# Delta-net heads: tiles in the order q, k, v, z, convolution taps read from PSUM, two value heads solved in turn, x normalised before its split

## The reference, cut to what matters

```
h      = rms_norm(x, norm_g)                      # x * rsqrt(mean x^2 + eps) * gain, per token
proj   = h @ dn_w_in                              # q, k (12 heads), v, z (24 heads), a, b, xq
qkv    = silu(causal_depthwise_conv(proj[q,k,v])) # 4 taps along the tokens, per channel
q, k   = l2_norm(q) / sqrt(128), l2_norm(k)       # each q/k head serves two value heads
g,beta = -exp(a_log)*softplus(a+dt), sigmoid(b)
o      = gated_delta_rule(q, k, v, g, beta)       # per value head: a unit lower triangular
                                                  # system per chunk, then a scan over chunks
mix    = rms_norm(o, out_g)
xa     = memory_cross_attention(xq, rms_norm(mem) @ w_kv)      # 4 heads
x      = x + (concat[mix, xa] * silu(z)) @ w_out
second layer: rms_norm, an mLSTM (4 heads), an HGRN (8 heads), out, a gated embedding, rms_norm
```

## Time and profile before

| what | us |
|---|---|
| median of 3 runs (range) | 3907.66 (3907.61 to 3908.97) |
| the profiled execution's own time | 3906.5 |
| its span, first to last instruction | 3904.6 |
| PE busy | 3431.5 (88%) |
| DVE, ACT, POOL busy | 1650.8, 782.0, 1839.2 |
| mean granted clock of PE | 0.949 |
| memory tiles (PE) | 36.1 to 140.1 |
| tile W_AB (PE) | 182.6 to 194.1 |
| cross-attention tiles | 210.4 to about 434 |
| first six delta tiles end | 500.3 |
| `natural` of head 0, head 1, head 11 starts | 506.4, 647.8, 1979.1 |
| end of `head_out` of head 11 (PE) | 2117.6 |
| tile W_GATE ends, first mLSTM tile starts | 2449.0, 2468.6 |

### The profile page before, as it was taken

One profiled execution on the slowest core, in us unless ns is written; L12 is line 12 of the kernel. 1 busy time (PEld: TensorE's weight loads), 2 busy tenths in 40 slices (PEclk: granted clock), 3 DMA queues, 4 the chain that ended last, 5 costly groups with the idle time before them and its releaser, 6 DMA issues.

```text
span 3904.6 us, 46749 instructions
## 1 busy us (share of the span) xinstructions
PE 3431.5 (88%) x17262; PEld 2836.3 (73%) x17262; DVE 1650.8 (42%) x2050; ACT 782.0 (20%) x1129; POOL 1839.2 (47%) x1828
## 2 busy tenths in 40 slices
PE   7789988898898889888969999799998888869897
PEld 6567777787777778777848777677776666648685
DVE  2422245544544553555352122334446565541433
ACT  3321122212211221222130001111122222220111
POOL 5444633433433433343324666466664444427574
PEclk9999999999999999999989999899999999989998
DMA  4312211111111111111122323122221111132222
GB/s 159 135 71 86 81 60 65 54 46 60 61 48 52 64 54 48 59 54 64 48 98 92 134 87 139 62 90 91 97 103 62 62 64 62 56 127 94 78 86 86
DMA packets 53362, 306.67 MB, mean 79 GB/s; under 512 B 5012, under 2 KB 7188, under 8 KB 21812
## 3 DMA queue, kind: packets, MB, share of 16 engines
q1 hardware_dynamic: 33984, 247.48, 18.0%
q10 hardware_dynamic: 19316, 58.32, 4.0%
HBM read 284.74 MB, written 21.04 MB: 78 GB/s over the span
## 4 chain that ended last, share of the span: by engine, by line
PE 72%; DVE 19%; issue 3%; ACT 3%; POOL 1%; DMA 1%; ACTq 0%; DVEq 0%; SPq 0%; POOLq 0%
PE gemm_ps L382 18%; PE gemm_ps L384 17%; PE gemm_ps L383 17%; DVE arena L761 14%; DVE arena L767 4%; PE bankA L494 4%; PE bankC L506 3%; PE bankB L504 2%; PE bankA L667 2%; ACT arena L1384 1%; POOL w_lo L340 1%; DVE a_lo L761 1%; PE bankA L529 1%; PE bankB L518 1%; PE bankA L513 1%
## 5 line engine op out<-in xcount | busy, mean ns | idle before, releaser
L382 PE MATMUL gemm_ps<-a_hi,w_hi 128*128 128x512 f32 (+1 forms) x3744 | 1512.6, 404 | 90.5 <-DVE a_lo L761 72.9
L355 POOL CAST w_hi<-w_raw 128x512 fp32r<-128x512 f32 x880 | 565.6, 684 | 1969.5 <-issue 1950.6
L383 PE MATMUL gemm_ps<-a_lo,w_hi 128*128 128x512 f32 (+1 forms) x3744 | 1452.0, 388 | 0.0
L384 PE MATMUL gemm_ps<-a_hi,w_lo 128*128 128x512 f32 (+1 forms) x3744 | 1451.3, 388 | 0.0
L340 POOL TENSOR_TENSOR w_lo<-w_raw,w_hi 128x512 fp32r<-128x512 f32 x944 | 1281.5, 1388 | 53.3 <-ACT w_hi L1384 53.3
L382 PEld LDWEIGHTS gemm_ps<-a_hi,w_hi 128*128 128x128 f32 x3744 | 719.5, 192 | 254.3 <-DVE a_lo L761 67.4
L384 PEld LDWEIGHTS gemm_ps<-a_hi,w_lo 128*128 128x128 f32 x3744 | 716.1, 191 | 145.3
L383 PEld LDWEIGHTS gemm_ps<-a_lo,w_hi 128*128 128x128 f32 x3744 | 718.8, 192 | 133.5 <-issue 9.9
L761 DVE TENSOR_TENSOR arena<-gemm_ps,arena 128x512 f32<-128x512 f32 (+3 forms) x234 | 157.5, 673 | 1043.5 <-PE gemm_ps L384 1018.7
L1384 ACT ACTIVATE arena<-arena 128x512 f32<-128x512 f32 (+5 forms) x418 | 252.3, 604 | 915.7 <-DVE arena L761 888.1
L761 DVE TENSOR_TENSOR arena<-arena 128x256 f32<-128x256 f32 (+3 forms) x444 | 331.8, 747 | 80.0 <-ACT arena L1618 43.6
(11 more groups left out here) (136 smaller groups left out, 2021.9 us busy)
## 6 DMA issues: line engine op xcount, KB each, us to landing
w_raw<-w_stream SPq DMA_DIRECT2D x236, 1024.0 KB, 4.8
y_scratch<-arena ACTq DMA_DIRECT2D x20, 512.0 KB, 3.2
arena<-y_scratch ACTq DMA_DIRECT2D x15, 512.0 KB, 3.6
arena<-gc_scratch ACTq DMA_DIRECT2D x12, 512.0 KB, 3.6
arena<-x_t ACTq DMA_DIRECT2D x1, 4096.0 KB, 15.3
arena<-y_scratch ACTq DMA_DIRECT2D x1, 4096.0 KB, 24.3
x_scratch<-arena ACTq DMA_DIRECT2D x1, 4096.0 KB, 12.1
y_out<-arena ACTq DMA_DIRECT2D x4, 1024.0 KB, 3.9
```

The costliest lines, as they stand in the source:

```text
L355: pool.tensor_copy(part(w_hi, w, q), part(w_raw, w, q)).then_inc(pool_step, 1)
L382: pe.matmul(o, hi, a_hi[:, k, 0:width], start=(k == 0), stop=False)
L383: pe.matmul(o, hi, a_lo[:, k, 0:width], start=False, stop=False)
L384: last = pe.matmul(o, lo, a_hi[:, k, 0:width], start=False, stop=(k == KT - 1))
```

## The change

1. **Loop order and weights of the steps.** The tiles of a head come as q, k, v, v, z, z (`stream`). `DN_STEPS` has new weights, `natural` is split (the transposes of v are a step `values` of their own, behind `gate` and all four `silu`; `natural` itself waits only for q and k and for `o_root` of the head before), and each level is four steps of weight 0.75: `half` and `whole` of value head 0 and of value head 1 in turn, with ACT copies of 128x512 and COPY_PREDICATED of 128x512. `head_out` starts at part 68 in place of 79. `qd` is made at the end of DVE's `natural`.
2. **Read-out.** For q, k, v ACT reads the PSUM tile and writes it times the last tap into `cv`; DVE adds three taps with SCALAR_TENSOR_TENSOR that read PSUM directly (`raw`, its copy and the TENSOR_SCALAR are gone); only then is the bank `evicted`; ACT's `Silu` follows. Tile q's first ACT copy waits for `pm_ready` of the solve beside it. z (here and in cross attention) is read by ACT's `Silu` straight from PSUM. `z_g` is a copy of `z_in` at the trip's end. The Sqrt table is asked for early in two places.
3. **x.** It is loaded after the memory's squares; its 16 squares (ACT) and their running sum `root` (DVE) go among memory tiles 7 to 14; one matmul with ones into bankC, root and reciprocal follow after the last memory tile; `fill(1)` multiplies gain and reciprocal root in one operation, so tiles of this layer need no `rstd` (`copied` in place of `scaled`). `square_sums(1)` is gone.
4. **Row transposes.** L421 and its copy move from behind W_AB to `q_norm` of the first cross-attention head; L597 and its copy from behind W_GATE to behind the first eight mLSTM tiles, and there PE waits for the copy.

```diff
-DN_STEPS = ([("natural", 14), ("transposed", 6)]
-            + [(s, l, g) for l in range(1, LEVELS) for s, g in (("half", 2.5), ("whole", 4))]
-            + [("solved", 4)]
-            + [(s, n, g) for n in range(NB) for s, g in (("rest", 2), ("output", 2))]
-            + [("head_out", 17)])
+X_FROM = 7
+DN_STEPS = ([("natural", 10), ("values", 8), ("transposed", 6)]
+            + [(s, l, a, 0.75) for l in range(1, LEVELS) for s in ("half", "whole") for a in range(2)]
+            + [("solved", 6)]
+            + [(s, n, g) for n in range(NB) for s, g in (("rest", 2), ("output", 3))]
+            + [("head_out", 28)])
...
-        ort, yo = halves(o_ + 5 * 1024), halves(o_ + 6 * 1024)
+        ort, yo = halves(o_ + 3 * 1024), halves(o_ + 5 * 1024)
...
+        def level_count(j, l, a):
+            return 2 * ((LEVELS - 1) * j + l - 1) + a + 1
...
+            pe.wait_ge(s["x_acc"], KT)
+            pe.matmul(bankC[:, 1, :], ones, root, start=True, stop=True).then_inc(s["sq_summed"], 1)
...
-            pe.wait_ge(s["kv_root"], XH)
-            square_sums(1)
             for k in range(KT):
                 gemm(W_AB, 0, k, 1)
-            pe.wait_ge(s["rows_ready"], 1)
...
                 if step[0] == "natural":
-                    pe.wait_ge(s["silu"], 4 * j + 4)
+                    pe.wait_ge(s["o_root"], 2 * j + 2)
+                    pe.wait_ge(s["silu"], 4 * j + 2)
...
+                elif step[0] == "values":
+                    pe.wait_ge(s["gate"], j + 1)
+                    pe.wait_ge(s["silu"], 4 * j + 4)
...
                 elif step[0] == "half":
+                    l, a = step[1:3]
+                    if l > 1:
+                        pe.wait_ge(s["lvl"], level_count(j, l - 1, a))
...
                 elif step[0] == "whole":
+                    pe.wait_ge(s["t1_sbuf"], level_count(j, l, a))
...
             ml_trip(0, None, mix=False)
+            pe.wait_ge(s["g_x"], 4)
...
+            last.then_inc(s["g_rowsT"], 1)
+            pe.wait_ge(s["mcols_ready"], 1)
             with pe.Fori(0, MLH - 1) as j:
...
                 scaled(kv[:, c, :], W_MEM, c, width=M)
+                if X_FROM <= c < X_FROM + KT // 2:
+                    for k in range(2 * (c - X_FROM), 2 * (c - X_FROM) + 2):
+                        v.wait_ge(s["squared"], KT + k + 1)
+                        if k == 0:
+                            op(v.tensor_copy, root, sqr[:, 0, :], sem=s["x_acc"], value=1)
+                        else:
+                            op(v.tensor_tensor, root, root, sqr[:, k % 2, :], ALU.add, sem=s["x_acc"], value=k + 1)
+            v.wait_ge(s["root_ready"], 2)
+            op(v.reciprocal, root, root, sem=s["rstd_ready"], value=2)
...
+            fill(1, src0, C_NORM, scale=root)
...
             def dn_evict(c, g):
-                scaled(raw[:, 3:T + 3], W_DN, c, g, 6)
-                o = cv[:, c - 2, :]
-                tap = 4 * (c - 2)
-                op(v.tensor_scalar, o, raw[:, 0:T], cw[:, tap:tap + 1], None, ALU.mult)
+                v.wait_ge(s["tapped"], 4 * g + c + 1)
+                tap = 4 * c + 3
                 for t in range(1, 4):
-                    op(v.scalar_tensor_tensor, o, raw[:, t:t + T], cw[:, tap + t:tap + t + 1], o, ALU.mult, ALU.add,
-                       sem=s["conv"] if t == 3 else None, value=4 * g + c - 1)
+                    o = cv[:, c, t:T]
+                    op(v.scalar_tensor_tensor, o, gemm_ps[slot][:, 0:T - t], cw[:, tap - t:tap - t + 1], o,
+                       ALU.mult, ALU.add, sem=evicted[slot] if t == 3 else None, value=n + 1)
...
                 elif step[0] == "whole":
+                    if l < LEVELS - 1:
+                        copy_after(v.copy_predicated, X[:, a, :, :], low[:, l:l + 1, :].to_broadcast([P, NB, P]),
+                                   quad(bankB)[:, a, :, :])
+                    copy_after(v.copy_predicated, XT[:, a, :, :], lowT[:, l:l + 1, :].to_broadcast([P, NB, P]),
+                               quad(bankC)[:, a, :, :], sem=s["lvl"], value=level_count(j, l, a))
...
+            act.dma_start(src0, xT).then_inc(s["src_loaded"], 16)
+            act.wait_ge(s["sq_summed"], KT)
+            for t in range(2, W_AB):
+                high_tile(t)
+                if X_FROM <= t < X_FROM + KT // 2:
+                    act.wait_ge(s["src_loaded"], 32)
+                    for k in range(2 * (t - X_FROM), 2 * (t - X_FROM) + 2):
+                        if k >= 2:
+                            act.wait_ge(s["x_acc"], k - 1)
+                        op(sqr[:, k % 2, :], src0[:, k, :], ACT.Square, s["squared"], KT + k + 1)
+            act.wait_ge(s["x_acc"], KT)
+            act.wait_ge(s["sq_summed"], KT + 1)
+            op(root, bankC[:, 1, :], ACT.Sqrt, s["root_ready"], 2, bias=eps[:, :], scale=1.0 / D)
...
             def gates(g):
+                op(z_g[:, :, :], z_in[:, :, :], ACT.Copy, s["gate"], g + 1)
+                act.preload_act_table(ACT.Sqrt)
...
                 elif step[0] == "half":
+                    act.wait_ge(s["t1"], level_count(j, l, a))
+                    if (l, a) == (1, 0):
+                        act.wait_ge(s["dy_stored"], 16 * j + 16)
+                    op(T1[:, a, :, :], quad(bankA)[:, a, :, :], ACT.Copy, s["t1_sbuf"], level_count(j, l, a))
                 elif step[0] == "head_out":
+                    act.preload_act_table(ACT.Sqrt)
                     act.wait_ge(s["o"], j + 1)
...
             def dn_trip(g, j, mix=True):
+                    if step[0] == "evict":
+                        act.wait_ge(gemm_done[slot], n + 1)
+                        if c >= 4:
+                            op(z_in[:, c - 4, :], gemm_ps[slot][:, :], ACT.Silu, evicted[slot], n + 1)
+                            continue
+                        act.wait_ge(s["taps"], g + 1)
+                        if mix and c == 0:
+                            act.wait_ge(s["pm_ready"], j + 1)
+                        o = cv[:, c, :]
+                        op(o, gemm_ps[slot][:, :], ACT.Copy, s["tapped"], 4 * g + c + 1, scale=cw[:, 4 * c + 3:4 * c + 4])
+                        act.wait_ge(evicted[slot], n + 1)
+                        op(o, o, ACT.Silu, s["silu"], 4 * g + c + 1)
...
-        stream += [z_t[2 * h:2 * h + 2], q_t[h:h + 1], k_t[h:h + 1], v_t[2 * h:2 * h + 2]]
+        stream += [q_t[h:h + 1], k_t[h:h + 1], v_t[2 * h:2 * h + 2], z_t[2 * h:2 * h + 2]]
```

More of the change, by code:

```diff
@@ L778, in reciprocal_root, with copied, fill @@
                 op(v.reciprocal, rstd[:, 0:width], root[:, 0:width], sem=s["rstd_ready"], value=q + 1)
-            def fill(f, src, gain, width=T, blocks=KT):
+            def copied(dst, base, c, i=0, per=0, rows=P):
+                slot, n = tile_at(base, c, i, per)
+                v.wait_ge(gemm_done[slot], n + 1)
+                op(v.tensor_copy, dst, gemm_ps[slot][0:rows, :], sem=evicted[slot], value=n + 1)
+            def fill(f, src, gain, width=T, blocks=KT, scale=None):
                 for w in range(2):
@@ L786, in product @@
                 def product(k):
+                    if scale is not None:
+                        op(v.scalar_tensor_tensor, stage[:, k % 4, 0:width], src[:, k, :], gains(gain + k), scale,
+                           ALU.mult, ALU.mult, sem=s["staged"], value=KT * GAINED[f] + k + 1)
+                        return
                     op(v.tensor_scalar, stage[:, k % 4, 0:width], src[:, k, :], gains(gain + k), None, ALU.mult,
@@ L1183, in _ @@
             ml_trip(0, None, mix=False)
+            v.wait_ge(s["g_rowsT"], 1)
+            op(v.tensor_copy, at(20992, NB * MLH), bankB[:, 0, 0:NB * MLH], sem=s["mcols_ready"], value=1)
+            d.wait()
             with v.Fori(0, MLH - 1) as j:
@@ L1423, in _ @@
             squares_and_high(0, 0, src_mem, M)
-            for t in range(2, W_AB):
-                high_tile(t)
             act.wait_ge(s["squared"], KT)
@@ L1522, in dn_mix @@
                     op(kroot, kss, ACT.Sqrt, s["k_root"], j + 1, bias=eps[:, :])
+                    op(q_sq, cv[:, 0, :], ACT.Square, scale=P * EPS ** 0.5)
+                elif step[0] == "values":
                     act.wait_ge(s["nat_v"], j + 1)
```

148 lines of the change are left out of this document (62 added, 86 removed).

## The result

| | before | after |
|---|---|---|
| median (range), us | 3907.64 (3907.23 to 3908.97) | 3768.94 (3767.43 to 3771.63) |
| ratio, 95% interval | | 0.9645 [0.9634, 0.9656] |
| span of the profiled execution | 3904.6 | 3769.8 |
| PE busy | 3431.5 | 3412.2 |
| memory tiles end | 140.1 | 159.8 |

What follows compares the result with a forecast made beforehand. PE, busy 88%, was taken as the bound, its longest wait at `natural` set by DVE's queue. Loop -142.7, head 11 -7, front -12 and mLSTM -19 make -180.7 from 3906.5: 3727 us forecast, range 3695 to 3800.

Steps and rivals of the forecast that it cites:

- Steady trips: Loop trips after the first: 113.7 us of PE work plus 2.8, 2.7, 1.0 and 0.3, in sum 120.5 each.
- The new wait at `head_out`: End of the loop trip: PE waits 2.7 us for ACT's square behind v1's read-out, plus 1.0 for half clock.
- The levels: Solve levels in the loop, value heads in turn: waits of 2.8 us a trip against 3.15 before.
- 1.5 us to spare: Loop, `pm_ready`: DVE done at 13.3 us, ACT's copy of tile q wants it at 14.8; cost nothing, a thin cover.
- First trip: First loop trip: waits of 3.1, 2.4 and 2.8 us from a late ACT queue, 2 for clock: 131 us.
- Memory stage: Memory tiles 9, 11, 13, 15 each delayed about 3.0 us by the squares of x: +12, bounds 0 and 16.
- W_AB and the first cross-attention tiles: Front after the memory tiles: -6.5 for W_AB inside the fill, -15.6 for L421's wait, -1.7 of half clock.
- Head 11: Last head beside w_out: a 5.4 us wait between y's 14th and 15th part and about 1.6 of half clock go: -7.
- mLSTM: mLSTM start: L597's 19.1 us wait and about 2.7 of half clock go, 2.3 and 0.5 come back: -19.
- dearer hand-overs: Rival, loop: taps at 1.2 to 1.66 beside POOL or no cover at `pm_ready`, +33 to +66, 3775 us; chance 0.20.
- Slower: Rival, solve levels: the two value heads do not overlap, 22 us a trip, 260 in all, 3985 us; chance 0.04.
- Table loads: Rival, `head_out`: each table switch keeps ACT busy another 1.4 us, wait 4.1 a trip, +15, 3742 us; chance 0.03.

Runs made afterwards that it cites:

- e1: The changed kernel with the step `transposed` (copy of X) ahead of tile q's read-out on PE and ACT, on DVE behind q's taps: 3769.2 us, ratio 0.9637.
- e9: The changed kernel with ACT's silus of q and k moved behind the copy at `solved`, those of v to the first z tile's read-out: 3715.5 us, ratio 0.9504.
- e12: e10 with the levels of both value heads together again and the old weights for levels, scan and `head_out`: 3698.5 us, ratio 0.9465.
- e3: The changed kernel without the early request for the Sqrt table at `head_out`: 3735.1 us, ratio 0.9554.
- e5: The kernel before with only the new tile order q, k, v, v, z, z and two waits that keep banks B and C apart: 3915.6 us, ratio 1.0017.
- e11: The kernel before with the new tile order, as in e5, and the silus late, as in e9: 3779.4 us, ratio 0.9672.
- e7: The changed kernel with DVE first copying the PSUM tile of q, k, v to SBUF and its taps reading that copy: 3892.2 us, ratio 0.996.
- e10: The changed kernel with silus late, DVE's adds of x's squares ahead of the memory tile's read-out, mLSTM row transposes behind the fourth tile: 3691.8 us, ratio 0.9451.
- e2: The changed kernel with `head_out` at part 73 in place of 68, by the weights of the last `output` and `head_out`: 3716.5 us, ratio 0.9504.
- e8: The changed kernel with the mLSTM gate rows' transposes and DVE's copy of them behind the fourth of eight mLSTM tiles, not the eighth: 3769.7 us, ratio 0.9642.

## Why the prediction was right, and where it was off

Direction and mechanism held; 42 us are missing. All large terms but one came out dearer than forecast, and the time is inside the range because that was wider towards slower times (73 us) than towards quicker ones (32). In the profiled executions -180.7 was forecast and -134.8 measured. By its own steps:

- **Steady trips: 120.5 forecast, 122.9 measured (+24 in ten).** The new wait at `head_out` came as worked out (2.7; 2.64, released by ACT's square), its half clock at 1.7 and not 1.0. The levels came as forecast too: 1.8 of idle in six gaps, and 0.16 at each by which a start lags the modelled end, 2.8. The step that failed is the one costed at nothing: "1.5 us to spare" at `pm_ready`. It came 15.0 us after natural's start (871.13), not 13.3, and DVE's copy of the taps' weights (L913) behind it, so q's copy was late (886.69, +15.6). The forecast had named what would follow ("ACT is late for `X`, and `half` waits") and priced it at nothing: X stands behind q's copy, taps, table and silu, and `half` waits 1.31, or 1.5 with its hand-over (PE's start after the release). With the 0.7 of half clock that is 2.2 of the 2.4. I had listed ACT's queue for v1 in full and not for q. e1 shows that moving X does not mend it, e9 that moving the silu takes 0.4 us off it and leaves 0.93 that DVE's queue holds. DVE at that place (the first line ends in `pm_ready`):

```profile
884.93 1.23 DVE L770 TENSOR_TENSOR arena<-arena 128x1024 f32<-128x1024 f32 x1
886.43 0.23 DVE L913 COPY arena<-par 128x16 f32 x1 [0.27 <-DVE arena L770]
```

- **First trip: 131 forecast, 134.4** (2.8, 2.3 and 4.1 where I had 3.1, 2.4 and 2.8).
- **Memory stage: +12 forecast, 16 at most, +19.7 measured (forecast end 152: 159.8), 20.1 of it in tiles 8 to 15.** The delay is sized rightly: PE's waits for `w_lo` rose from 15.8 to 28.1, by 12.3. What I left out is what such waits bring: tiles 8 to 15 ran at a clock of 0.88, with four stretches at 0.5 (17.1 us, worth at most half of that) where before there was none, and that is the other 7.8. I had charged half clock to waits in the loop, and not here.

```profile
88.50:159.81 71.31, 54.94 (x384) 53.52 (x385) 21.43 (x23) 22.23 (x21) 44.36 (x36) 0.88 0.33 118
```

- **W_AB and the first cross-attention tiles: -24 forecast, -29.** W_AB ends 44.5 behind the memory tiles (47.5 forecast, 53.6 before); the transposes hide as said; another 1.7 is a half-clock stretch (3.4 us at 292.3 before) gone in a later head. No run has the normalisation or the row transposes of part 3 and 4 by themselves, so these terms are read from the trace of the whole change.
- **Head 11: -7 forecast, +0.7.** The end of `head_out` comes 6.8 earlier, but the step was moved 11 parts ahead in the list, 33 matmuls or 7.5 us, which PE now does behind it. To the end of w_out (L596, L588 before) the stretch is 445.0 for 444.2. A stage must be cut at the same work, not at the same step. Neither term of the forecast came. The wait of 5.4 left its place, but PE's waits for the parts of y, before and after (total, times, longest), are as long as they were:

```profile
PE gemm_ps L382 <- DVE a_lo L761: 23.5, 7, 10.1
PE gemm_ps L385 <- DVE a_lo L770: 23.8, 7, 14.3
```

The longest, ahead of the first part, took it up, and the first tile ends 47.5 us after natural's start where it was 45.5. And half clock did not shrink by 1.6: it is granted for 34.1 us up to the end of `head_out`, for 23.3 before (clock 0.87 for 0.92).
- **mLSTM: -19 forecast, -10.8.** L597's 19.1 went. But DVE's gate chain was not "2 us ahead" of tile 2's bank: PE waits 3.3 there, with 5.6 us at half clock behind it (2.8), and the eight small operations behind the copy at the scores ran at half clock, 2.9 longer (0.5 forecast). Both lines of that stretch, total, times, longest:

```profile
PE gemm_ps L385 <- DVE arena L770: 3.3, 1, 3.3
PE bankB L612 <- DVE arena L770: 2.7, 1, 2.7
```

Of the rivals, "dearer hand-overs" (0.20) is the one nearest in number (3775) and partly in kind: the thin cover was gone, while the taps took 0.75 exactly as read from the earlier trace rows. "Slower" is refuted in its mechanism by 19.5 us of level waits in all, and e12 shows that even whole levels do not cost that. "Table loads" is refuted by e3.

What I credited to the order of tiles was not its own. e5 gains nothing, e11 gains 122 in the loop, the change as made 110, and e9 167. So the order opens room at the trip's end, and whether the room is used is decided by what ACT's silu, standing in its queue until DVE's taps are done, holds back. Two ways to use it were shown. The change shortened what the silu waits for (with the taps back in SBUF, e7, the loop is 122 us longer), and moving the silus gets more in the loop with the old, long read-out left as it was (e11).

Left open: whether e11 with the earlier `rest` read-out and parts 3 and 4 would pass e10; whether silus late (e9) and `head_out` at part 73 (e2), each worth about 53 us, add anything to each other; and what the order with taps from PSUM, and nothing else, is worth. None of these was run.

## What to carry to other kernels

In an in-order queue, an instruction that waits for another engine holds all behind it: put the last, unhurried step of a read-out (here a silu whose result is not needed for at least 35 us) where its input has long been there, before anything is shortened. When one item behind such a holder is late, list all of them; moving one only passes the wait on. And compare stages between points that have the same work ahead of them.

## What the runs showed of the hardware

- The wait of 2.64 us at `head_out` was followed by 3.41 us at the lower clock level in every steady trip, the one of 1.42 us (e3) by none; so 1.2 us less of waiting was worth 2.9. The length of one wait does not tell it alone: in the first trip of the changed kernel a wait of 2.80 (503.0) had full clock behind it, and the one of 2.29 that came 9 us later (511.9) had 3.41 us at half.
- A gain of 4.7 us was undone by where half clock fell later in one pair of traces (e8), with no change to the work; in another pair (e9, e10) 4.6 us were gained at the same place and 1.1 lost behind it.
- DVE's taps: 0.75 from PSUM in all 144 cases, whatever POOL did. In SBUF 0.75 with POOL idle (the three under e5: 2.33 with the steps between them), 0.86 to 0.95 under its CAST, 1.63 to 1.88 under its TENSOR_TENSOR (e7).
